# Gate-weight residuals on GpSimd in 1024-wide instead of 256-wide instructions, and one Newton step of a norm moved one head earlier on VectorE

## The chip, the cores and the metric

The kernel runs on one core of a Trainium2 chip. The metric is the device time of one execution in microseconds (us). The profile and the trace are those of one execution; engines are PE (TensorE), DVE (VectorE), ACT (ScalarE), POOL (GpSimd) and SP (SyncE, which issues most of the DMAs).

## The reference

Two trunk layers run over 128 context tokens and 512 latent tokens (640 in all, width 1024). What matters here is the middle of a layer:

```
g = sigmoid(h @ w_gate + b_gate)            # 1024 -> 4 x 1024, four branches
oa = diff_attn(q, ka, va, lam, sa)          # branch A: 4 heads, two score maps each
oa = rms_norm(oa, a_subln_g) * (1 - lam_init)   # per head, over 64 values
ob = neighborhood_attn(...)                 # branch B: 4 heads
oc = softmax_attn(...)                      # branch C: 4 heads
merged = g[0]*oa@a_wo + g[1]*ob@b_wo + g[2]*oc@c_wo + g[3]*od
x += gate1 * (merged @ w_out);  then a mixture of experts, top 2 of 16
```

## The kernel before

The order of the work on each engine is written out by hand; semaphores connect the engines. A float32 matmul is done as three float16 passes (`passes`, L430): each float32 operand is split into a high half (the cast to float16) and a low half (the float32 minus the high half). For a weight block of 128 x 2048 ACT makes the high half (`whi`, in two casts of 1024, L1360), and POOL makes the low half (`wlo`) with `low`: `wlo = wf - whi`, L1719. The operands all lie in SBUF. `low` cuts a block into pieces of `piece` columns and signals `w_lo` after the last; the default is 1024, and the calls for the gate weights pass `piece=256`.

The gate projection has 16 units of 2048 columns a layer (`GATE_UNITS`). It gives 13 such calls a layer on POOL in 256-wide pieces (units 3 to 15). The two buffers `whi` and `wlo` alternate: when PE has finished a unit, ACT casts the unit after the next one into the buffer that came free, and POOL follows.

The gate matmuls are laid out between the attention heads as filler for PE. A tile of 128 query tokens has 12 heads (`HDS`): heads 0 to 3 of branch A with two maps each, then one map for each of heads 4 to 11. The tiles go in the order 1, 2, 3, 4, 0; tile 0 is the context, with 128 keys instead of 640. `GATE_SETS` gives each step `g` (one head) 8 or 4 sets of three passes, 64 a latent tile, which are two gate units. So POOL's blocks fall on the same two places in every latent tile: one in its first heads, one in its later heads.

A step `g` of PE in the later heads of a tile: scores of the next pair of heads (`scores`, L1033), the transposes of the weights of head g-1 (`turn`, L1049), their product with V (`values`), gate sets. `turn` waits for `pt_ready` of the head before, which DVE gives with L2150.

The step `g` of DVE from head 4 on, in this order: `maxima(g + 1)` (L2165, a reduce over PSUM), `weights_turned(g - 1)` (L2150, the low half of the transposed weights, one operand in PSUM), `sub_norm(g - 2)`, `sums(g)` (L2183, a reciprocal). `sub_norm` is the RMS norm of branch A, spread over five heads: head 5 forms the sums of squares, head 6 a first estimate of 1/sqrt and a Newton step, heads 7 and 8 a Newton step each, head 8 the product (L2228), head 9 the gain (L2232). A Newton step (`root_step`) has three instructions on 128 x 4 values in SBUF, L2203, L2205 and L2207, with a drain behind each. In the first heads of a tile `sums` also has L2187 (one column) and L2193 (128 x 640, `wmix`), both with two inputs in SBUF.

The convolution early in a layer (L1999, 128 x 655, both inputs in SBUF) runs on DVE beside `low` in its default pieces of 1024.

Of the kernel before, what the change touches and what calls it, by code (L numbers as in the profile page):

```python
# [47 lines left out]
V_GATE = V_IN + IN_UNITS  # L48
V_WO = V_GATE + GATE_UNITS
V_OUT = V_WO + 2  # L50
V_ALL = V_OUT + OUT_UNITS
# [31 lines left out]
def build(nc, t):  # L83
    ctx = ExitStack()
    with ctx:
# [354 lines left out]
        def ran_before(eng):  # L440


            b, ran = (eng.value_load(loopi[0:1, n:n + 1], min_val=0, max_val=LAYERS * (PAIRS + 1)) for n in (0, 2))
            return b, ran, b + ran
# [12 lines left out]
        def head(g):  # L457

            if not 0 <= g < HEADS_ALL:
                return None  # L460
            ti, hd = divmod(g, HDS)
            return ti, ORDER[ti], hd, ((2 * hd, 2 * hd + 1) if hd < 4 else (hd + 4,))
# [1246 lines left out]
        @block.gpsimd  # L1709
        def _(pool):  # L1710
            for l in range(LAYERS):
                def low(count, j, dst=None, n=2048, piece=1024):

                    pool.wait_ge(w_hi.sem, count)
                    hi = (whi[j] if dst is None else dst[0])[:, 0:n]
                    lo = (wlo[j] if dst is None else dst[1])[:, 0:n]
                    for a in range(0, n, piece):
                        b = min(a + piece, n)
                        ins = pool.tensor_tensor(lo[:, a:b], wf[j][:, a:b], hi[:, a:b], ALU.subtract)  # L1719
                    ins.then_inc(w_lo.sem, 1)  # L1720

                pool.wait_ge(*w_lo(l, V_IN + 2))
                for u in range(2, IN_UNITS):
                    low(l * V_ALL + (V_IN + u + 1), u % 2, n=2048 if u < IN_UNITS - 1 else KC * 160)

                low(l * V_ALL + (V_GATE + 1), 0)
                for n in range(1, TILES):
                    if n >= 3:
                        low(l * V_ALL + (V_GATE + n - 1), (n - 2) % 2)
                    if n == 1:  # L1730
                        pool.wait_ge(*proj_ready(l, 40))
                        pool.wait_ge(*cv_var(l, 1))
                    else:
                        pool.wait_ge(*ab_t(l, 2 * n - 1))
                    v = proj[:, n, 0:512].rearrange("p (h n) -> p h n", n=32)
                    r2 = rope2.rearrange("p (h n) -> p h n", n=32)
                    for o, i in ((0, 8), (8, 0), (16, 24), (24, 16)):
                        pool.tensor_tensor(r2[:, :, o:o + 8], v[:, :, i:i + 8],
                                           sinb[:, n - 1:n, o:o + 8].to_broadcast([P, 16, 8]), ALU.mult)
                    pool.drain()  # L1740
                    pool.tensor_tensor(v, v, cosb[:, n - 1:n, :].to_broadcast([P, 16, 32]), ALU.mult)
                    pool.drain()
                    pool.tensor_tensor(roped.rearrange("p (h n) -> p h n", n=32), v, r2, ALU.add).then_inc(roped_ready.sem, 1)
                low(l * V_ALL + (V_GATE + 4), 1, piece=256)
                with pool.Fori(0, GATE_UNITS // 2 - 2) as i:
                    for j in range(2):
                        low(l * V_ALL + i * 2 + (V_GATE + j + 5), j, piece=256)
                for b in (2, 3, 0, 1):
                    flat = [w[:, b, :, :].rearrange("p k n -> p (k n)") for w in (wohi, wolo)]
                    if b < 2:  # L1750
# [20 lines left out]
                b, ran, past = ran_before(pool)  # L1771
# [30 lines left out]
                for tile in range(TILES):  # L1802
                    for ch, dst in enumerate((cga, cgb)):
                        n = ch * TILES + tile
# [6 lines left out]
        def _(dve):  # L1811
# [62 lines left out]
            def bc(ap, shape):  # L1874
                return ap.to_broadcast(shape)
# [91 lines left out]
            for l in range(LAYERS):  # L1967
# [229 lines left out]
                def root_step(first):  # L2197

                    x, y, t2 = ostat[:, 0, :], ostat[:, 1, :], ostat[:, 2, :]
                    if first:  # L2200
                        dve.tensor_scalar(y.bitcast(I32), x.bitcast(I32), -0.5, 1597463007.0, ALU.mult, ALU.add)
                        dve.drain()
                    dve.tensor_tensor(t2, y, y, ALU.mult)  # L2203
                    dve.drain()
                    dve.scalar_tensor_tensor(out=t2, in0=t2, scalar=-0.5, in1=x, op0=ALU.mult, op1=ALU.mult)  # L2205
                    dve.drain()
                    dve.scalar_tensor_tensor(out=y, in0=t2, scalar=1.5, in1=y, op0=ALU.add, op1=ALU.mult)  # L2207
                    dve.drain()

                def sub_norm(g):  # L2210

                    ti, _, hd, _ = head(g)
                    oa = otok[:, ti % 2, 0:256].rearrange("p (h n) -> p h n", h=4)
                    if hd == 5:
                        dve.wait_ge(*o_ready(l, ti * HDS + 4))
                        dve.tensor_tensor(osq, otok[:, ti % 2, 0:256], otok[:, ti % 2, 0:256], ALU.mult)
                        dve.drain()
                        dve.tensor_reduce(ostat[:, 2, :], osq.rearrange("p (h n) -> p h n", h=4), AX_X, ALU.add)
                        dve.drain()
                        dve.tensor_scalar(ostat[:, 0, :], ostat[:, 2, :], 1.0 / 64, EPS, ALU.mult, ALU.add)  # L2220
                        dve.drain()
                    elif hd == 6:
                        root_step(True)
                    elif hd == 7:
                        root_step(False)
                    elif hd == 8:
                        root_step(False)
                        dve.tensor_tensor(oa, oa, bc(ostat[:, 1, :].rearrange("p (h o) -> p h o", o=1), [P, 4, 64]),  # L2228
                                          ALU.mult)
                        dve.drain()  # L2230
                    elif hd == 9:
                        dve.tensor_tensor(oa, oa, bc(rowg[:, 0:64].rearrange("p (o n) -> p o n", o=1), [P, 4, 64]),  # L2232
                                          ALU.mult).then_inc(on_ready.sem, 1)

                for g in range(-1, HEADS_ALL + 4):
                    last_turned = head(g - 4) and head(g - 4)[2] == HDS - 1
                    if g % HDS < 4:
                        if head(g):
                            sums(g)
                        if last_turned:  # L2240
                            rows_turned(*head(g - 4)[:2])
                        if head(g + 1):
                            maxima(g + 1)
                        if head(g - 1):
                            weights_turned(g - 1)
                    else:
                        if head(g + 1):
                            maxima(g + 1)
                        if head(g - 1):
                            weights_turned(g - 1)  # L2250
                        if head(g - 2):
                            sub_norm(g - 2)
                        if head(g):
                            sums(g)
                    if g > HEADS_ALL:
                        wo_low((2, 3, 0)[g - HEADS_ALL - 1])
# [107 lines left out]
                b, ran, past = ran_before(dve)  # L2364
# [75 lines left out]
                for n, sh in enumerate((1, 2, 4, 8)):  # L2440
                    a, o = csum[n % 2], csum[1 - n % 2]
# [98 lines left out]
                with dve.Fori(0, p + 1) as i:  # L2540
                    for n in range(2):
                        c, j = i * 2 + (1 + n), 1 - n
# [128 lines left out]
```

## Time and profile before

| | us |
|---|---|
| median of 3 runs | 1917.68 |
| lowest, highest | 1914.58, 1923.54 |
| the profiled execution | 1923.54 |
| its span | 1921.7 |

Busy in the span: PE 86%, DVE 63%, ACT 47%, POOL 24%. The mean granted TensorE clock is 0.925 of full speed. A row of the time-ordered view has start, length, engine, line, operation, written and read tiles, and in brackets how long the engine had been idle and who released it. PE's busy time is matmul time; rows of one instruction can overlap a little with the next. An idle engine costs nothing unless it is the one that others end up waiting for.

### The profile page before, as it was taken

What the parts mean: (1) busy time and instruction counts of PE and PEld (TensorE: products, weight loads), DVE (VectorE), ACT (ScalarE), POOL (GpSimd) and SP (SyncE); (2) the same over time, 40 slices, a digit from 0 to 9 for tenths busy, and PEclk for the clock granted to TensorE, in tenths of its full rate; (3) what the DMA queues carried; (4) which work ended last, traced back from release to release, by engine and by line L of the source; (5) the groups of instructions that cost most, each with busy time, mean ns of one, the idle gap of its engine ahead of it and who ended that gap; (6) DMA issues with size and microseconds to landing.
All of it is one profiled execution on the core that took longest, in us unless ns stands there. A gap on an engine that the chain in (4) does not pass through costs nothing.

```text
span 1921.7 us, 34497 instructions
## 1 busy us (share of the span) xinstructions
PE 1657.3 (86%) x13277; PEld 1114.3 (58%) x13277; DVE 1206.4 (63%) x1888; ACT 904.5 (47%) x1478; POOL 455.7 (24%) x430
## 2 busy tenths in 40 slices
PE   6799889999989886888679998999999989288877
PEld 4478766777665443434356876677776546244436
DVE  4595355777438448777575916477773664777754
ACT  3322545666541124777532235466664221376753
POOL 0032252222242023212202315322223121322111
PEclk7899999999999997999869999999999999699995
DMA  8555235532327466999634622322223643399954
GB/s 294 180 198 168 70 130 187 183 106 70 114 96 253 155 244 223 361 373 356 246 117 145 240 85 90 99 100 72 72 79 125 214 150 110 135 356 352 376 216 161
DMA packets 191107, 350.71 MB, mean 183 GB/s; under 512 B 15478, under 2 KB 98935, under 8 KB 190711
## 3 DMA queue, kind: packets, MB, share of 16 engines
q1 hardware_dynamic: 181647, 319.58, 47.5%
q0 software_dynamic: 7776, 28.32, 4.0%
q8 instruction: 97, 1.59, 0.3%
q10 hardware_dynamic: 1543, 0.88, 0.2%
q14 instruction: 44, 0.35, 0.1%
HBM read 287.72 MB, written 61.01 MB: 181 GB/s over the span
## 4 chain that ended last, share of the span: by engine, by line
PE 63%; DVE 12%; DMA 10%; ACT 5%; issue 5%; DVEq 2%; SPq 1%; another core or an unknown queue 0%; ACTq 0%; POOL 0%; POOLq 0%
PE PS L430 36%; PE PS L437 10%; DMA wf<-in_moe_w 4%; DMA arena<-in_moe_w 4%; PE PS L1049 3%; PE PS L1033 3%; PE PS L851 2%; DVE arena L2369 2%; PE PS L807 1%; DMA wf<-in_w_out 1%; PE PS L833 1%; PE PS L817 1%; ACT arena L1615 1%; ACT arena L1433 1%; DVE hpart L1868 1%
## 5 line engine op out<-in xcount | busy, mean ns | idle before, releaser
L1719 POOL TENSOR_TENSOR wlo<-wf,whi 128x256 f16<-128x256 f32 (+1 forms) x268 | 278.3, 1071 | 926.4 <-ACT whi L1360 926.4
L430 PE MATMUL PS<-hpart,whi 128*128 128x320 f16 x2048 | 425.5, 301 | 16.9 <-ACT arena L1433 15.9
L430 PE MATMUL PS<-hpart,wlo 128*128 128x320 f16 x1024 | 307.6, 300 | 0.0
L430 PE MATMUL PS<-whi,hpart 128*128 128x256 f16 (+2 forms) x1568 | 298.3, 291 | 5.9 <-DVE scratch L1989 3.6
L430 PEld LDWEIGHTS PS<-hpart,whi 128*128 128x128 f16 x2048 | 191.2, 98 | 105.9 <-issue 34.9
L430 PE MATMUL PS<-wlo,hpart 128*128 128x256 f16 (+2 forms) x784 | 225.9, 291 | 0.0
L430 PEld LDWEIGHTS PS<-whi,hpart 128*128 128x128 f16 x1568 | 151.9, 98 | 65.3 <-issue 24.1
L2369 DVE TENSOR_TENSOR arena<-arena 128x2048 f16<-128x2048 f32 x66 | 149.5, 2288 | 41.0 <-ACT arena L1615 41.0
L2165 DVE TENSOR_REDUCE stat<-PS 128x1 f32<-128x640 f32 (+1 forms) x160 | 110.7, 713 | 79.7 <-PE PS L1033 77.3
L1433 ACT ACTIVATE arena<-PS,pcol 128x320 f32<-128x320 f32 x128 | 67.5, 527 | 171.8 <-PE PS L430 166.6
L1999 DVE SCALAR_TENSOR_TENSOR scratch<-scratch,cw 128x655 f32<-128x655 f32 x120 | 138.8, 1198 | 4.8 <-issue 0.4
L1615 ACT CAST arena<-arena 128x2048 f16<-128x2048 f32 x66 | 123.4, 1897 | 33.0 <-DMA arena<-in_moe_w 33.0
L1360 ACT CAST whi<-wf 128x1024 f16<-128x1024 f32 (+1 forms) x84 | 109.8, 1307 | 54.1 <-DMA wf<-in_w_out 35.0
L1523 ACT ACTIVATE scratch<-PS,stat 128x640 f32<-128x640 f32 (+1 forms) x160 | 113.0, 709 | 39.2 <-DVE stat L2165 38.5
L430 PEld LDWEIGHTS PS<-hpart,wlo 128*128 128x128 f16 x1024 | 100.6, 98 | 39.8
L2150 DVE TENSOR_TENSOR arena<-PS,arena 128x640 f16<-128x640 f32 (+1 forms) x120 | 85.6, 714 | 49.4 <-ACT arena L1542 46.3
L2369 DVE TENSOR_TENSOR wlo<-wf,whi 128x2048 f16<-128x2048 f32 x36 | 82.3, 2291 | 40.7 <-ACT whi L1615 39.4
L1542 ACT CAST arena<-PS 128x640 f16<-128x640 f32 (+1 forms) x120 | 72.8, 607 | 57.0 <-PE PS L1049 56.8
L430 PE MATMUL PS<-arena,hpart 128*128 128x512 f16 x384 | 95.6, 402 | 4.0 <-issue 3.6
L1398 ACT COPY arena<-PS 128x256 f32<-128x256 f32 (+1 forms) x80 | 28.8, 360 | 144.9 <-PE PS L430 144.9
L430 PE MATMUL PS<-arena,scratch 128*128 128x512 f16 x408 | 93.6, 379 | 2.8 <-DVE scratch L2526 2.8
L437 PE MATMUL PS<-arena,whi 128*128 128x128 f16 (+1 forms) x512 | 91.5, 302 | 0.0
(351 smaller groups left out, 2861.3 us busy)
## 6 DMA issues: line engine op xcount, KB each, us to landing
arena<-in_moe_w SPq DMA_DIRECT2D x66, 1024.0 KB, 8.5
arena<-in_w_ada SPq DMA_DIRECT2D x40, 1024.0 KB, 7.2
wf<-in_moe_w SPq DMA_DIRECT2D x36, 1024.0 KB, 10.2
wf<-in_w_gate SPq DMA_DIRECT2D x32, 1024.0 KB, 5.5
g_rows<-arena SPq DMA_DIRECT2D x128, 160.0 KB, 1.8
wf<-in_w_in SPq DMA_DIRECT2D x18, 1024.0 KB, 7.8
y_rows<-scratch SPq DMA_DIRECT2D x34, 512.0 KB, 9.0
arena<-g_rows SPq DMA_DIRECT2D x24, 640.0 KB, 5.1
```

Of the source, the lines that this page charges most:

```text
L430: ins = pe.matmul(out, st, mv, start=first and n == 0, stop=last and n == 2)
L437: ins = pe.matmul(pr(pair)[:, a:b], st, mv[:, a:b], start=first and n == 0, stop=last and n == 2)
L1360: return act.copy(whi[j][:, a:b] if dst is None else dst, wf[j][:, a:b])
L1433: act.activation(sg(n), bank(7, 320), ACT.Tanh, scale=0.5, bias=pcol[:, PC_BG + u % 4 * 8 + d:PC_BG + u % 4 * 8 + d + 1]).then_inc(g_ready ...
L1523: act.activation(ex[:, m % 4, 0:nk], pr(m % 2)[:, 0:nk], ACT.Exp, bias=stat[:, 0, m:m + 1], accum_out=stat[:, 1, m:m + 1]).then_inc(ex_rea ...
L1542: act.copy(pthi[:, hd % 2, 0:nk], pr(2)[:, 0:nk]).then_inc(pt_hi.sem, 1)
L1615: act.copy(mwhi[3 * j + q], mwf[3 * j + q]).then_inc(mw_hi.sem, 1)
L1719: ins = pool.tensor_tensor(lo[:, a:b], wf[j][:, a:b], hi[:, a:b], ALU.subtract)
L1999: ins = dve.scalar_tensor_tensor(out=zacc[:, c, :], in0=zpad[:, c, k:k + NZ], scalar=cw[:, c, k:k + 1], in1=zacc[:, c, :], op0=ALU.mult, o ...
L2150: dve.tensor_tensor(ptlo[:, hd % 2, 0:nk], pr(2)[:, 0:nk], pthi[:, hd % 2, 0:nk], ALU.subtract).then_inc(pt_ready.sem, 1)
L2165: dve.tensor_reduce(stat[:, 0, m:m + 1], pr(m % 2)[:, 0:nk], AX_X, ALU.max, negate=True).then_inc(mx_ready.sem, 1)
L2369: dve.tensor_tensor(mwlo[3 * j + q], mwf[3 * j + q], mwhi[3 * j + q], ALU.subtract).then_inc((mw_lo2 if q == 2 else mw_lo).sem, 1)
```

## The change

`low` loses its parameter: all pieces are 1024 wide, so a gate unit takes two POOL instructions instead of eight. And the Newton step of head 8 is done in head 7, behind the one that is there, so that head 7 has six small instructions and head 8 none besides the product.

```diff
-                def low(count, j, dst=None, n=2048, piece=1024):
+                def low(count, j, dst=None, n=2048):
...
-                    for a in range(0, n, piece):
-                        b = min(a + piece, n)
+                    for a in range(0, n, 1024):
+                        b = min(a + 1024, n)
                         ins = pool.tensor_tensor(lo[:, a:b], wf[j][:, a:b], hi[:, a:b], ALU.subtract)
...
-                low(l * V_ALL + (V_GATE + 4), 1, piece=256)
+                low(l * V_ALL + (V_GATE + 4), 1)
                 with pool.Fori(0, GATE_UNITS // 2 - 2) as i:
                     for j in range(2):
-                        low(l * V_ALL + i * 2 + (V_GATE + j + 5), j, piece=256)
+                        low(l * V_ALL + i * 2 + (V_GATE + j + 5), j)
...
                     elif hd == 7:
                         root_step(False)
+                        root_step(False)
                     elif hd == 8:
-                        root_step(False)
                         dve.tensor_tensor(oa, oa, bc(ostat[:, 1, :].rearrange("p (h o) -> p h o", o=1), [P, 4, 64]),
                                           ALU.mult)
```

## Rows read from the trace of the kernel before

**Rows 1.** The page: busy time, and the chain that ended last.

```profile
PE 1657.3 (86%) x13277; PEld 1114.3 (58%) x13277; DVE 1206.4 (63%) x1888; ACT 904.5 (47%) x1478; POOL 455.7 (24%) x430
...
PE 63%; DVE 12%; DMA 10%; ACT 5%; issue 5%; DVEq 2%; SPq 1%; another core or an unknown queue 0%; ACTq 0%; POOL 0%; POOLq 0%
```

**Rows 2.** One tile's stretch: length, busy time and count of PE, PEld, DVE, ACT, POOL; clock.

```profile
394.36:442.74 48.38, 47.55 (x538) 34.30 (x537) 36.13 (x69) 32.54 (x69) 10.73 (x17) 1.00 0.25 83
```

**Rows 3.** Instructions in time order, second latent tile, heads 7 and 8 of the norm.

```profile
394.36 5.08 POOL L1719 TENSOR_TENSOR wlo<-wf,whi 128x256 f16<-128x256 f32 x8 [20.11 <-ACT whi L1360]
...
395.94 0.36 DVE L2203 TENSOR_TENSOR ostat<-ostat 128x4 f32<-128x4 f32 x1
...
396.38 0.56 DVE L2205 SCALAR_TENSOR_TENSOR ostat<-ostat 128x4 f32<-128x4 f32 x1
397.01 0.55 DVE L2207 SCALAR_TENSOR_TENSOR ostat<-ostat 128x4 f32<-128x4 f32 x1
...
397.64 0.16 DVE L2183 RECIPROCAL stat<-stat 128x1 f32<-128x1 f32 x1
...
398.44 0.81 DVE L2150 TENSOR_TENSOR arena<-PS,arena 128x640 f16<-128x640 f32 x1
399.17 0.28 DVE L2203 TENSOR_TENSOR ostat<-ostat 128x4 f32<-128x4 f32 x1
399.40 0.74 PE L1049 MATMUL PS<-ident,scratch 128*128 128x128 f32 x5 [0.28 <-DVE arena L2150]
...
399.52 0.16 DVE L2205 SCALAR_TENSOR_TENSOR ostat<-ostat 128x4 f32<-128x4 f32 x1
399.76 0.16 DVE L2207 SCALAR_TENSOR_TENSOR ostat<-ostat 128x4 f32<-128x4 f32 x1
```

**Rows 4.** The same for lines L1999 and L1719, around 1034 us.

```profile
L1999 DVE SCALAR_TENSOR_TENSOR scratch<-scratch,cw x120: 886/902/2840, 100.1 to 1104.8; 128x655 f32<-128x655 f32 x120
...
L1999 DVE SCALAR_TENSOR_TENSOR scratch<-scratch,cw x1: 2607/2607/2607, 1034.2 to 1034.2; 128x655 f32<-128x655 f32 x1
L1719 POOL TENSOR_TENSOR wlo<-wf,whi x2: 2290/2505/2720, 1033.9 to 1036.1; 128x1024 f16<-128x1024 f32 x2
L1999 DVE SCALAR_TENSOR_TENSOR scratch<-scratch,cw x1: 2757/2757/2757, 1036.8 to 1036.8; 128x655 f32<-128x655 f32 x1
```

**Rows 5.** A block in two 1024-wide pieces with DVE out of the way.

```profile
L1719 POOL TENSOR_TENSOR wlo<-wf,whi 128x1024 f16<-128x1024 f32 x2 | 4.2, 2128 | 14.8 <-ACT whi L1360 14.8
```

**Rows 6.** Time order, the other block of the tile, first heads.

```profile
416.97 5.65 POOL L1719 TENSOR_TENSOR wlo<-wf,whi 128x256 f16<-128x256 f32 x8 [17.54 <-ACT whi L1360]
...
420.88 1.22 DVE L2193 SCALAR_TENSOR_TENSOR scratch<-scratch,cfa 128x640 f32<-128x640 f32 x1
421.36 0.80 ACT L1532 CAST arena<-PS 128x768 f16<-128x768 f32 x1
422.19 0.96 DVE L2173 TENSOR_TENSOR arena<-PS,arena 128x768 f16<-128x768 f32 x1
```

**Rows 7.** Time order, the first heads of the context tile.

```profile
511.71 5.12 POOL L1719 TENSOR_TENSOR wlo<-wf,whi 128x256 f16<-128x256 f32 x8 [15.51 <-ACT whi L1360]
...
515.79 0.96 DVE L2173 TENSOR_TENSOR arena<-PS,arena 128x768 f16<-128x768 f32 x1 [1.37 <-ACT arena L1532]
```

**Rows 8.** Time order, head 7 of the last latent tile of layer 0.

```profile
491.12 5.07 POOL L1719 TENSOR_TENSOR wlo<-wf,whi 128x256 f16<-128x256 f32 x8 [20.11 <-ACT whi L1360]
...
494.75 0.16 DVE L2183 RECIPROCAL stat<-stat 128x1 f32<-128x1 f32 x1 [0.42 <-issue]
```

**Rows 9.** Stretches around two pauses of PE (columns as in rows 2).

```profile
252.68:254.95 2.27, 0.00 (x1) 0.01 (x1) 2.19 (x9) 2.24 (x3) 0.23 (x1) 1.00 0.29 88
254.95:258.00 3.05, 3.05 (x25) 2.54 (x26) 3.05 (x7) 2.11 (x7) 1.91 (x4) 1.00 1.00 305
...
264.47:267.30 2.83, 0.00 (x0) 0.00 (x1) 2.75 (x8) 0.53 (x1) 1.13 (x1) 1.00 0.49 195
267.30:271.10 3.80, 3.80 (x18) 2.95 (x19) 3.39 (x7) 1.77 (x5) 2.28 (x5) 0.57 0.09 36
```

## The prediction

> **What bounds the kernel now.** I read the page first [rows 1]. PE is busy for 86% of the span and has 63% of the chain that ended last; POOL, whose instructions the change rewrites, has 0% of that chain, and DVE, where the other edit is, has 12%. So a cheaper POOL buys nothing by itself, and DVE counts only where PE waits for it. Next I took the busy time by stretches over the attention heads, where the 256-wide pieces lie. One latent tile takes 48.38 us and PE is busy for 47.55 us of them [rows 2]; the same stretch repeats within 0.1 us through both layers. PE has 0.83 us of idle time a tile: little to win, and no room to absorb a new stall. Then I read one such tile in time order. POOL makes two blocks a tile at fixed places: one just before heads 7 and 8 of the norm [rows 3], one in the first heads of the next tile [rows 6].
>
> What to see in rows 3: the three instructions of a Newton step (L2203, L2205, L2207) handle 4 values a partition and take 0.16 us each when POOL is quiet, 0.24 us from start to start (the pair at 399.52 and 399.76). While POOL runs they take 0.36, 0.56 and 0.55 us and end at 396.30, 396.94 and 397.56. POOL's eight pieces take 5.08 us, one each 0.63 us, and the third, fourth and fifth end at about these three times. Each tiny instruction has waited for the piece that was running, and POOL had started the next piece before the following one could go. Instructions with one operand in PSUM (L2150, 0.81 us) show no such wait.
>
> **Does the wait grow with the piece?** The convolution shows it, for there the pieces are already 1024 wide [rows 4]. L1999 takes 0.90 us alone. The one at 1034.24 takes 2.61 us, beside a piece that runs from 1033.86 for 2.29 us; the next takes 2.76 us, beside the second piece, which ends at 1038.85. So a DVE instruction waits for a whole 1024-wide piece, and POOL's second piece gets in ahead of the second DVE instruction. The Trainium skill, SBUF — State Buffer, section "SBUF: two separate sides", says this as a rule: the port pair that DVE and GpSimd share is an exclusive lock, held for the whole instruction, and a DVE instruction with two SBUF inputs needs it against a GpSimd one that reads SBUF. By that rule, the trace agrees. It speaks against this change; if the loser only shared bandwidth, four times the piece would cost DVE nothing more and the sum below would be near zero.
>
> **The change part by part.**
>
> POOL's work: a block goes from 5.08 us in eight pieces to 4.2 us in two of 2.13 us that end 4.2 us after the first starts [rows 5]. That is 0.9 us on each of 26 blocks. PE needs a block only when it has used up the other buffer, half a tile (24 us) later, and the loads that the block's end releases are as far ahead. I cost this at nothing; the cover is those 24 us.
>
> Wider pieces with the moved step, at the seven ordinary places (four latent tiles in two layers make eight; the last of layer 0 comes below). I take POOL's start of rows 3, since ACT's cast that releases it stands in ACT's own order just ahead of the cast that leads to L2150. Piece one ends at 394.36 + 2.13 = 396.49. L2203, issued at 395.94, ends with it: 396.50. Piece two runs until 394.36 + 4.2 = 398.56. L2205 is issued at 396.6 and ends with that: 398.57. L2207 ends 0.24 us later, at 398.81 (before: 397.56, so 1.25 us later from the width alone). Then come three more instructions, 3 x 0.24 = 0.72 us: 399.53. The reciprocal L2183 starts 0.08 us after that as it does now: at 399.61 instead of 397.64, 1.97 us late.
>
> Who waits for that: behind it in DVE's order stand the next reduce and L2150, which ended at 399.25 and would now end at 401.22. PE's transposes L1049 at 399.40 had already waited 0.28 us for it, so nothing covers the delay: PE stalls 1.97 us more. Head 8's step is indeed shorter by its three instructions (0.28 + 0.24 + 0.24 us), but they stood behind L2150, in a stretch where PE was not waiting for DVE; taking them from there returns nothing, while in head 7 they stand in front. 7 x 1.97 = 13.8 us.
>
> The eighth place [rows 8]: L2183 had an idle 0.42 us in front of it. By the same count it starts at 491.12 + 5.25 = 496.37 instead of 494.75: 1.6 us.
>
> The other block of the latent tiles [rows 6]: the one-column L2187 just ahead of L2193 waits in both versions, now for piece two, which ends at 416.97 + 4.2 = 421.17. L2193 then runs unhindered from 421.25, some 0.9 us as L1999 of nearly the same width does [rows 4], until 422.15 (before: 420.88 + 1.22 = 422.10). L2173 behind it also waits for ACT's cast, which ends at 422.16. So L2173 and the PE transposes that wait for it move by 0.05 us: six places, 0.3 us.
>
> The context tile's first heads [rows 7]: L2187 ends with piece one, at 513.84, and L2193 with piece two, 511.71 + 4.2 = 515.91, plus about 0.2 us; L2173 moves from 515.79 to about 516.15, and PE waits for it: 2 x 0.35 = 0.7 us.
>
> The remaining eight blocks (in each layer the last two, and two at the beginning of the heads) meet DVE where it idles in between, or where fewer waits and longer ones cancel. A wait of 0.4 us, as L2205 has now over its 0.16 us, can go or come at each: within 3 us either way in all; I take zero.
>
> Sum: 13.8 + 1.6 + 0.3 + 0.7 = 16.4 us. The profiled execution took 1923.54 us with a span of 1921.7, so it would take 1939.9. It was the slowest of the three, 5.9 us over the median; against the median I predict 1917.68 + 16.4 = 1934.1 us, 0.86% more.
>
> What is not in the trace: six tiny instructions in a row beside 1024-wide pieces. The lower bound is one waited piece instead of two, 1 us in all (rival C works it out); a gain is excluded, for the first wait and the six instructions stand on the path in any case. The upper bound is both pieces as priced and 0.2 us more at each place, as L2193 and the second L1999 end some way behind their piece: 18 us. I take the two pieces, for the rows nearest to it, rows 3 for the size of the instruction and rows 4 for the size of the piece, show every instruction waiting.
>
> **The rivals.**
>
> A. Forecast: each of two tiny instructions waits for a whole piece, PE stalls; 1934.1.
>
> B. The same, and PE's clock falls. PE would pause for 0.28 + 1.97 = 2.25 us each time. In one place PE pauses for 2.27 us and the granted clock stays 1.00; in another it pauses for 2.83 us and the clock is then 0.57 over 3.80 us (the 1.2 GHz level for most of it) [rows 9], a loss of 3.80 x 0.43 = 1.6 us. Eight such losses add 13 us: 1947. For it: 2.25 lies not far under the pause that cost clock. Against: the pause of 2.27 us is as long and did no harm. The Trainium skill, TensorE: Matmul & The Clock Gate, section "What's actually happening", says that the clock goes by how busy the array has been recently, so the same pause can fare differently by what stands around it; by that rule some of the eight could pay.
>
> C. DVE gets its second instruction in before POOL's second piece. Then only L2203 waits for piece one (396.50), the other five take 5 x 0.24 = 1.2 us and are through at 397.70, against 397.56 now: 0.14 us a tile, 1 us in all, so not slower. It decides at the gap between two pieces: L2205 must be ready within it. Against: L2205 now comes 0.08 us behind L2203's end and yet waits for a whole piece each time [rows 3], as does the second L1999 [rows 4]. Time: 1919.
>
> D. PE doesn't pay in full, since a later wait of PE shrinks in turn. It could give back at most its 0.83 us of idle time a tile: 16.4 - 8 x 0.83 = 9.8 us, 1927.5. If more of the delay falls where PE has other work in front of it, down to 1922.
>
> E. Faster, since DVE loses fewer waits in all: bounded by PE's idle 0.83 us a tile, eight tiles, 6.6 us or 0.35%. It can't pass 0.5%.
>
> **How the numbers follow.** A 0.60, B 0.13 (with some of the eight places paying), C 0.09, D 0.15, E 0.03. A change under 0.5% (9.6 us) is about what a measurement of this kernel can't tell from none. A's own range, with its bounds and the spread of the medians, is 1929 to 1940. The whole range, from D's lower part to the smaller half of B, is 1922 to 1943. Slower by over 0.5%: A and B and a good part of D, less A's chance to be measured low: 0.78. Within: C and the rest of D: 0.19. Faster: 0.03.
>
> **What would show it.** In the profile of the changed kernel: L1719 with 26 x 2 = 52 instructions of 1024 where there were 208 of 256; in rows like rows 3, L2203 at about 0.55 us and the L2205 behind it at about 2.0 us, then four at 0.16; L1049 with an idle time of about 2.2 us released by L2150; a tile of 50.4 us with PE's busy time still 47.55 and the clock 1.00. If L2205 there takes 0.16 us, C is right; if L1049's idle time stays under 1 us, D; if the clock in these tiles is under 1.00, B. The prediction is wrong above all if POOL's start moves against L2203 by more than 0.5 us, for then the tiny instructions meet only one of the pieces.

## The result, and the profile after

The changed kernel takes 1948.40 us (median of 4 runs, 1934.07 to 1952.65), the kernel before 1919.99 us (median of 4). The ratio is 1.0138, with a 95% interval of 1.0098 to 1.0178: slower, by about 26 us. All 21 recorded executions of the changed kernel have a median of 1945.89 us and reach from 1934.07 to 1961.12. The prediction was slower by 16.4 us, 1934.1 us with a range of 1922 to 1943. The direction was right, and the time lies above the range, by either median. The profiled execution took 1945.07 us, with a span of 1943.2.

The page of the kernel after: busy time and the chain that ended last. POOL has 25 us less work than in [rows 1], and L2205, an instruction on four values a partition, has 1% of the chain that ended last, and did not stand among its leading entries before.

```profile
PE 1672.5 (86%) x13277; PEld 1120.0 (58%) x13277; DVE 1220.6 (63%) x1888; ACT 904.7 (47%) x1478; POOL 430.2 (22%) x274
...
PE PS L430 36%; PE PS L437 10%; DMA arena<-in_moe_w 4%; DMA wf<-in_moe_w 3%; PE PS L1033 3%; PE PS L1049 3%; PE PS L851 2%; DVE arena L2369 2%; PE PS L807 1%; DMA wf<-in_w_out 1%; PE PS L833 1%; PE PS L817 1%; DVE ostat L2205 1%; ACT arena L1615 1%; ACT arena L1433 1%
```

The kernel after in time order, the same place as [rows 3]:

```profile
398.44 4.22 POOL L1719 TENSOR_TENSOR wlo<-wf,whi 128x1024 f16<-128x1024 f32 x2 [21.54 <-ACT whi L1360]
...
400.03 0.56 DVE L2203 TENSOR_TENSOR ostat<-ostat 128x4 f32<-128x4 f32 x1
...
400.67 2.01 DVE L2205 SCALAR_TENSOR_TENSOR ostat<-ostat 128x4 f32<-128x4 f32 x1
...
402.76 0.16 DVE L2207 SCALAR_TENSOR_TENSOR ostat<-ostat 128x4 f32<-128x4 f32 x1
402.99 0.16 DVE L2203 TENSOR_TENSOR ostat<-ostat 128x4 f32<-128x4 f32 x1
...
403.71 0.16 DVE L2183 RECIPROCAL stat<-stat 128x1 f32<-128x1 f32 x1
...
405.47 0.74 PE L1049 MATMUL PS<-ident,scratch 128*128 128x128 f32 x5 [2.25 <-DVE arena L2150]
```

This is the predicted picture to within 0.03 us: L2203 waits for piece one, L2205 for piece two, four instructions run free, the reciprocal starts 5.27 us after POOL's start (predicted 5.25), and PE's pause is 2.25 us (2.25 to 2.27 us at six of the eight places, 2.61 at two). So where does the rest come from? The stretches tell. In the rows below, each stretch runs from POOL's block in the later heads of a tile to the next block (columns as in [rows 2]); the eight such stretches of the kernel after:

```profile
346.48:372.68 26.20, 23.94 (x260) 17.41 (x258) 17.35 (x33) 15.14 (x33) 4.22 (x3) 0.93 0.42 147
...
398.44:423.04 24.60, 22.34 (x260) 16.44 (x258) 17.34 (x33) 15.04 (x33) 4.22 (x2) 1.00 0.27 92
423.04:448.81 25.77, 25.21 (x282) 17.87 (x279) 20.01 (x36) 17.51 (x37) 4.23 (x3) 1.00 0.21 68
448.81:476.64 27.83, 25.57 (x260) 18.00 (x258) 17.34 (x33) 15.14 (x33) 4.22 (x3) 0.88 0.20 62
...
502.40:526.54 24.14, 21.29 (x223) 15.70 (x222) 12.57 (x35) 11.95 (x34) 4.22 (x3) 0.93 0.32 101
...
1289.27:1314.23 24.96, 22.35 (x260) 16.43 (x258) 17.35 (x33) 15.04 (x33) 4.23 (x3) 1.00 0.23 70
...
1339.99:1367.75 27.76, 25.50 (x260) 18.08 (x258) 17.35 (x33) 15.14 (x33) 4.22 (x3) 0.88 0.20 63
...
1393.51:1421.36 27.85, 25.59 (x260) 17.66 (x258) 17.36 (x33) 15.04 (x33) 4.22 (x2) 0.88 0.20 63
...
1447.13:1469.35 22.22, 19.72 (x223) 15.05 (x222) 12.56 (x35) 11.95 (x34) 4.22 (x3) 1.00 0.38 125
```

The row at 423.04 is the other half of a tile, for comparison; before, it took 25.77 us too. The first and the last of the eight before:

```profile
345.98:368.59 22.61, 22.34 (x260) 16.43 (x258) 16.20 (x33) 15.04 (x33) 5.07 (x9) 1.00 0.48 170
...
1423.54:1443.77 20.23, 19.71 (x223) 15.04 (x222) 11.42 (x35) 11.94 (x34) 5.07 (x8) 1.00 0.42 137
```

With the clock at 1.00 a full stretch takes 24.60 us against 22.61: 1.99 us for the pause. With 0.93 it takes 26.20, 1.60 us more, with 0.88 it takes 27.8, 3.2 us more, and in these PE's busy time itself has grown, from 22.34 to 23.94 and 25.57 us for the same 260 matmul rows. The eight sum to 205.56 us against 176.51, 29.05 us more, and PE's busy time in them grew by 12.8 us. That is rival B, at five of the eight places. The span grew by 21.5 us only: single executions also differ elsewhere (the four of the kernel before range over 9 us and the profiled one was the slowest of them); the ratio says 26.

The two places with a pause of 2.61 us are the last of layer 0 and the first of layer 1. In each DVE has an idle time of about 0.42 us between two of the small instructions:

```profile
507.31 0.16 DVE L2203 TENSOR_TENSOR ostat<-ostat 128x4 f32<-128x4 f32 x1 [0.42 <-issue]
...
509.78 0.74 PE L1049 MATMUL PS<-ident,scratch 128*128 128x128 f32 x5 [2.61 <-DVE arena L2150]
...
1294.42 0.16 DVE L2205 SCALAR_TENSOR_TENSOR ostat<-ostat 128x4 f32<-128x4 f32 x1 [0.43 <-issue]
```

### The profile page after: what moved, and what is told of

Its sections match the earlier page's. It is cut to its first block, busy times and chain, and to the rows that moved or that the text cites. A ratio compares the mean times of both kernels' runs of the same rounds, so it can differ in the third digit from the quotient of the medians.

```text
span 1943.2 us, 34341 instructions
## 1 busy us (share of the span) xinstructions
PE 1672.5 (86%) x13277; PEld 1120.0 (58%) x13277; DVE 1220.6 (63%) x1888; ACT 904.7 (47%) x1478; POOL 430.2 (22%) x274
## 4 chain that ended last, share of the span: by engine, by line
PE 62%; DVE 13%; DMA 10%; ACT 6%; issue 5%; DVEq 2%; SPq 1%; POOL 0%; ACTq 0%; POOLq 0%
PE PS L430 36%; PE PS L437 10%; DMA arena<-in_moe_w 4%; DMA wf<-in_moe_w 3%; PE PS L1033 3%; PE PS L1049 3%; PE PS L851 2%; DVE arena L2369 2%; PE PS L807 1%; DMA wf<-in_w_out 1%; PE PS L833 1%; PE PS L817 1%; DVE ostat L2205 1%; ACT arena L1615 1%; ACT arena L1433 1%
## 5 line engine op out<-in xcount | busy, mean ns | idle before, releaser
L1719 POOL TENSOR_TENSOR wlo<-wf,whi 128x1024 f16<-128x1024 f32 x112 | 250.6, 2258 | 974.2 <-ACT whi L1360 974.2
L430 PE MATMUL PS<-hpart,whi 128*128 128x320 f16 x2048 | 431.7, 304 | 16.9 <-ACT arena L1433 15.9
L1999 DVE SCALAR_TENSOR_TENSOR scratch<-scratch,cw 128x655 f32<-128x655 f32 x120 | 138.8, 1198 | 4.8 <-issue 0.4
L2150 DVE TENSOR_TENSOR arena<-PS,arena 128x640 f16<-128x640 f32 (+1 forms) x120 | 85.6, 714 | 48.2 <-ACT arena L1542 45.1
L430 PE MATMUL PS<-arena,hpart 128*128 128x512 f16 x384 | 99.6, 415 | 4.0 <-issue 3.6
L1049 PE MATMUL PS<-ident,scratch 128*128 128x128 f32 x504 | 78.5, 281 | 24.8 <-DVE arena L2150 19.2
```

Source lines behind the costliest of these rows:

```text
L430: ins = pe.matmul(out, st, mv, start=first and n == 0, stop=last and n == 2)
L1049: ins = pe.transpose(pr(2)[:, c * P:(c + 1) * P], src[:, c * P:(c + 1) * P], ident[:, :])
L1999: ins = dve.scalar_tensor_tensor(out=zacc[:, c, :], in0=zpad[:, c, k:k + NZ], scalar=cw[:, c, k:k + 1], in1=zacc[:, c, :], op0=ALU.mult, o ...
L2150: dve.tensor_tensor(ptlo[:, hd % 2, 0:nk], pr(2)[:, 0:nk], pthi[:, hd % 2, 0:nk], ALU.subtract).then_inc(pt_ready.sem, 1)
```

## The experiments

In what follows "the eight stretches" are these, from POOL's block in the later heads to the next block; 176.51 us in the kernel before. They are those of one profiled execution of each kernel. Each ratio is against executions of the kernel before that were made together with that experiment's (medians 1916.18, 1916.86 and 1912.83 us).

**Wide pieces alone.**

```diff
 # against the changed kernel
                     elif hd == 7:
                         root_step(False)
-                        root_step(False)
                     elif hd == 8:
+                        root_step(False)
```

> Only the pieces are 1024 wide; head 8 keeps its Newton step. Theory (whole-piece waits, and a clock that falls only behind the longer pauses): L2203 about 0.56 us and L2205 about 2.0 us beside POOL, the reciprocal 1.25 us later than before, PE's pause ahead of L1049 0.28 + 1.25 = 1.53 us. A pause of 1.72 us in the kernel before cost no clock, so the clock stays 1.00 in these tiles: 8 x 1.25 + 1.0 = 11 us over the kernel before, ratio 1.006. Rival (the clock falls behind any new stall here): half of the eight places lose 1.6 us or more as well, 18 us or more, ratio 1.009 or more.

Measured: ratio 1.0062 (1.0030 to 1.0094). In time order:

```profile
396.03 2.01 DVE L2205 SCALAR_TENSOR_TENSOR ostat<-ostat 128x4 f32<-128x4 f32 x1
...
400.11 0.74 PE L1049 MATMUL PS<-ident,scratch 128*128 128x128 f32 x5 [1.54 <-DVE arena L2150]
```

The stretch of that place:

```profile
393.81:417.68 23.87, 22.33 (x260) 16.42 (x258) 17.33 (x33) 15.04 (x33) 4.21 (x2) 1.00 0.28 94
```

The pause is 1.54 us (1.90 at the last place of layer 0), the clock is 1.00 in all eight stretches, and they sum to 186.63 us, 10.1 more than before. That is as the theory had it: the width costs about 1.25 us a place and, in this execution, no clock.

**The moved step alone.**

```diff
 # against the kernel before
                     elif hd == 7:
                         root_step(False)
+                        root_step(False)
                     elif hd == 8:
-                        root_step(False)
```

> Only the Newton step is moved; the pieces stay 256 wide. Theory: six instructions wait for one piece each (0.63 us), the last for the eighth piece, 5.08 us after POOL's start: the reciprocal 1.9 us later than before, nearly the 1.97 of both parts together, PE's pause 2.15 us. So 8 x 1.9 = 15 us without any loss of clock (ratio 1.008), and up to 1.014 if the pause of 2.15 us costs clock as often as that of 2.25 us. Rival (the parts simply add, 0.72 us a place for the moved step): 6 us, ratio 1.003.

Measured: ratio 1.0154 (1.0118 to 1.0191).

```profile
402.57 0.55 DVE L2207 SCALAR_TENSOR_TENSOR ostat<-ostat 128x4 f32<-128x4 f32 x1
...
403.20 0.55 DVE L2203 TENSOR_TENSOR ostat<-ostat 128x4 f32<-128x4 f32 x1
403.82 0.56 DVE L2205 SCALAR_TENSOR_TENSOR ostat<-ostat 128x4 f32<-128x4 f32 x1
404.46 0.55 DVE L2207 SCALAR_TENSOR_TENSOR ostat<-ostat 128x4 f32<-128x4 f32 x1
...
406.84 0.74 PE L1049 MATMUL PS<-ident,scratch 128*128 128x128 f32 x5 [2.15 <-DVE arena L2150]
```

One of the stretches with a lower clock:

```profile
346.44:374.16 27.72, 25.56 (x260) 17.77 (x258) 17.24 (x33) 15.13 (x33) 5.08 (x8) 0.88 0.40 138
```

Each of the six waits for one piece; PE pauses 2.15 us, as expected, and the clock falls in seven of the eight stretches of the profiled execution, which sum to 32.5 us more. The ratio lies a little above the expected 1.008 to 1.014, and its interval covers the upper end. This one edit costs as much as both together: the two don't add. The rival of 0.72 us a place is out.

**The pause filled.** PE does matmuls while it would stand still; nothing reads their result.

```diff
 # against the changed kernel, PE, at the head step before L1049's late start
+                    if g % HDS == HDS - 1 and 0 < g < HEADS_ALL - HDS:
+                        pe.wait_ge(*ex_ready(l, g // HDS * MAPS + MAPS - 1))
+                        for _ in range(10):
+                            pe.matmul(PS[:, 0, 640:1024], hhi[:, 0, 0:P], hhi[:, 1, 0:384], start=True, stop=True)
```

> The changed kernel, and in the pause PE does ten matmuls of 384 columns (1.6 us at full clock) whose result nobody reads, ahead of L1049 in the four places of a layer. Theory (the 10 us above the predicted 16 are TensorE's clock): DVE's rows stay as they are, L1049 starts as late as in the changed kernel, the clock is 1.00 in all eight tiles, and the time is the predicted 16.4 us over the kernel before, ratio 1.0086, with a smaller spread between executions. Rival (the excess comes from another wait): ratio stays at 1.013 or goes above it.

Measured: ratio 1.0071 (1.0044 to 1.0099). In time order, and one stretch (the lines of DVE are 4 higher in this kernel):

```profile
400.05 1.79 PE L1068 MATMUL PS<-hpart 128*128 128x384 f16 x10
...
402.46 0.74 PE L1049 MATMUL PS<-ident,scratch 128*128 128x128 f32 x5 [0.63 <-DVE arena L2154]
```

```profile
445.80:470.39 24.59, 23.96 (x270) 17.41 (x268) 17.33 (x33) 15.02 (x33) 4.22 (x2) 1.00 0.22 71
```

L1049 starts as late after POOL's start as in the changed kernel (7.01 us against 7.03), but PE's idle time in front of it is down to 0.63 us (0.98 at two places), the clock is 1.00 in all eight stretches, and none takes over 24.94 us. They sum to 192.67 us, 16.16 more than before. So 16.2 us of the 29.05 are the pauses themselves and 12.9 us are the clock, which agrees with the 12.8 us by which PE's busy time had grown. Adding work to PE has taken 13 us away; the two ratios, 1.0138 and 1.0071, are as far apart.

**The pause half filled,** with four matmuls instead of ten.

```diff
 # against the kernel with the filled pause
-                        for _ in range(10):
+                        for _ in range(4):
```

> As the filled pause, with four of the unread matmuls (0.65 us) instead of ten, so that PE is idle for about 1.5 us of the pause, as with wide pieces alone, but DVE is as late as in the changed kernel. Theory (what counts is how long PE is idle, 1.5 us costs nothing): clock 1.00 in all eight stretches, each 24.60 us, ratio 1.007 to 1.009. Rival (half-filled pauses cost clock too): some stretches below 1.00 and over 26 us, ratio 1.011 or more.

Measured: ratio 1.0094 (1.0057 to 1.0132), with a clock of 1.00 in six stretches. In two, where DVE was some 0.35 us later than elsewhere, PE was idle for 1.96 and 1.95 us instead of 1.6, and the clock was 0.93 and 0.94. One of the two, the pause and what follows:

```profile
505.62:507.58 1.96, 0.00 (x1) 0.03 (x1) 1.89 (x5) 0.78 (x2) 0.00 (x0) 1.00 0.01 4
507.58:511.40 3.82, 3.81 (x36) 2.63 (x37) 2.49 (x10) 2.24 (x9) 0.00 (x0) 0.71 0.12 43
```

The expectation that half filling is enough held for the pauses of 1.6 us and failed for the two near 2, though the pause of 1.90 us with wide pieces alone had lost nothing. The ratio lies between the two expected ranges and its interval covers both.

**No Newton step in head 7, two in head 8.** Once with the wide pieces, once with the narrow ones.

```diff
 # against the kernel before; the wide version has the changed kernel's `low` as well
                     elif hd == 7:
-                        root_step(False)
+                        pass
                     elif hd == 8:
                         root_step(False)
+                        root_step(False)
```

> Pieces of 1024, head 7 without a Newton step, head 8 with two, behind L2150. Theory: no DVE instruction with two SBUF inputs is issued while POOL runs there, L1049's idle time goes from 0.28 (before) and 2.25 us (changed) to nearly 0, and two Newton steps (1.44 us) fit into DVE's idle time: the time is that of the kernel before or up to 4 us less, ratio 0.998 to 1.001. Rival (wide pieces cost by themselves, wherever the small instructions stand): ratio 1.005 or more.

> Pieces of 256 as before, head 7 without a Newton step, head 8 with two. Theory: head 7 has nothing that POOL can hold; the two steps of head 8 are issued when one or two pieces are still to come, behind L2150, where PE waits for nothing: the same stretches as with wide pieces and the late steps (22.15 us), ratio 0.998 to 1.001. Rival (narrow pieces are what protects DVE): a difference of over 2 us from the wide pieces with late steps, one way or the other.

Measured: ratio 0.9996 (0.9974 to 1.0018) with wide pieces, 1.0000 (0.9973 to 1.0027) with narrow ones. The stretch of the one and of the other:

```profile
440.61:462.75 22.14, 22.14 (x260) 16.51 (x258) 15.16 (x33) 15.02 (x33) 4.22 (x2) 1.00 0.25 78
```

```profile
439.57:461.71 22.14, 22.14 (x260) 16.50 (x258) 15.59 (x33) 15.02 (x33) 5.08 (x8) 1.00 0.24 78
```

PE is never idle in these two stretches, L1049's wait for L2150 is gone at all eight places, and both sum to 172.41 us, 4.1 less than before. In the time of the whole kernel that can't be told from nothing. With the steps placed there, the width of the pieces makes no difference, as the theory had it. By the ratios both versions are 1.4% under the changed kernel and can't be told from the kernel before.

**A third Newton step in head 7.** The norm gets one step more than it needs.

```diff
 # against the changed kernel
                     elif hd == 7:
                         root_step(False)
                         root_step(False)
+                        root_step(False)
```

> The changed kernel with one more Newton step in head 7 (three there; the result of the norm gets one step more than it needs). Theory: 0.72 us more DVE work in each of eight places, PE's pause about 2.97 us instead of 2.25. The kernel before had a pause of 2.83 us, and the clock fell behind it: so the clock falls at all eight places, not at five. 22 us of pauses and 8 x 1.6 to 3.3 us of clock: 35 to 48 us over the kernel before, ratio 1.018 to 1.025. Rival (what the clock does is chance, not tied to the pause's length): 5.8 us over the changed kernel, ratio 1.016 or 1.017, and about five places with a loss.

Measured: ratio 1.0187 (1.0131 to 1.0243), inside the expectation, but not for its reason. The pauses are 2.97 us as worked out (3.31 at one place), and the clock fell at four of the eight places only. The eight stretches sum to 30.7 us more than before, under the expected 35 to 48. One place where it did not fall:

```profile
404.75:407.72 2.97, 0.00 (x0) 0.03 (x1) 2.58 (x9) 0.78 (x2) 0.00 (x0) 1.00 0.00 0
407.72:411.50 3.78, 3.78 (x45) 2.70 (x46) 1.99 (x5) 2.15 (x7) 0.00 (x0) 1.00 0.12 43
```

So the theory that a longer pause costs clock for certain is wrong, and its rival, with about five places, is nearer. The ratio can't decide between them, as its interval covers the rival's 1.016 as well.

**Pieces of 512.**

```diff
 # against the changed kernel
-                    for a in range(0, n, 1024):
-                        b = min(a + 1024, n)
+                    for a in range(0, n, 512 if n == 2048 and dst is None else 1024):
+                        b = min(a + (512 if n == 2048 and dst is None else 1024), n)
```

> The changed kernel with pieces of 512 in all of GpSimd's blocks of whole weight units. Theory: six waiting instructions are held until the block is done whatever its cut is: L2203, L2205 and L2207 wait for pieces two, three and four of about 1.1 us each (estimate between the 0.63 us of a 256 and the 2.08 us of a 1024 piece), the last ends 4.5 us after POOL's start, the rest is free; PE's pause 2.2 to 2.35 us, ratio 1.010 to 1.016 as with 1024. Rival (a piece half as wide holds half as long): pause about 1.3 us and ratio 1.004.

Measured: ratio 1.0185 (1.0126 to 1.0244).

```profile
401.72 0.70 DVE L2203 TENSOR_TENSOR ostat<-ostat 128x4 f32<-128x4 f32 x1
...
402.50 1.04 DVE L2205 SCALAR_TENSOR_TENSOR ostat<-ostat 128x4 f32<-128x4 f32 x1
...
403.61 1.04 DVE L2207 SCALAR_TENSOR_TENSOR ostat<-ostat 128x4 f32<-128x4 f32 x1
...
407.20 0.74 PE L1049 MATMUL PS<-ident,scratch 128*128 128x128 f32 x5 [2.30 <-DVE arena L2150]
```

Three instructions wait for one piece each, the last until the block is done. The pause is 2.30 us, about that of 256 (2.15) and 1024 (2.25). The clock fell at all eight places here, and the stretches sum to 35.9 us more than before, so the ratio is above the expected range. (The edit also narrows POOL's blocks of 2048 columns outside the gate projection; the eight stretches hold only gate blocks.)

**The changed kernel profiled twice more,** with no edit.

> The changed kernel once more, unchanged, for one look. If the clock's losses are a matter of how the pause happens to lie, the eight stretches of the later heads lose at other places, and in another number, than in the first look (five of eight: 0.93, 1.00, 0.88, 0.93, 1.00, 0.88, 0.88, 1.00). If they are tied to the place and the length of the pause, the same five lose.

> The changed kernel a third time: as in the look before it. Chance: again another set of places. Tied to the place: the same set. In either case the pauses themselves are 2.25 us, and the time goes with the number of stretches at the lower clock, 1.6 us for each 3.4 us of it.

Measured: 1953.31 and 1941.99 us. The clock of the eight stretches, in order (four of layer 0, then four of layer 1):

| profiled execution | layer 0 | layer 1 |
|---|---|---|
| first | 0.93, 1.00, 0.88, 0.93 | 1.00, 0.88, 0.88, 1.00 |
| second | 0.93, 1.00, 0.88, 0.93 | 0.88, 0.88, 1.00, 1.00 |
| third | 1.00, 0.88, 0.88, 0.93 | 1.00, 0.88, 0.88, 1.00 |

Two of the changed places of the second execution, and two of the third:

```profile
1297.45:1325.60 28.15, 25.55 (x260) 18.10 (x258) 17.33 (x33) 15.12 (x33) 4.21 (x2) 0.88 0.20 62
...
1404.98:1429.57 24.59, 22.34 (x260) 16.43 (x258) 17.34 (x33) 15.03 (x33) 4.21 (x3) 1.00 0.23 71
```

```profile
344.30:368.89 24.59, 22.33 (x260) 16.43 (x258) 17.33 (x33) 15.04 (x33) 4.22 (x2) 1.00 0.45 156
...
394.66:422.48 27.82, 25.57 (x260) 18.03 (x258) 17.34 (x33) 15.14 (x33) 4.22 (x3) 0.88 0.25 82
```

Each execution has five places with a loss, but not the same five: four places lost in one execution and are clean in another. Neither expectation holds in full, though: the number was five each time, three places lost in all three executions and one in none, so the place may matter as well as chance. Three executions can't separate the two. The eight stretches sum to 29.0 and 30.8 us more than before. The pauses are the same each time. The expectation that the time goes with the number of these places was not borne out: these two sums differ by under 2 us and the times by 11, the other way round. The rest of the kernel varies as well; what varies there is not shown.

## Why the prediction was wrong, and where it was right

- *A DVE instruction waits for a whole piece, and POOL gets its next piece in first.* Right, with pieces of 256, 512 and 1024: a small instruction that meets a whole piece takes 0.55, 1.04 and 2.01 us instead of 0.16. By the rule of the Trainium skill (SBUF — State Buffer, "SBUF: two separate sides"), an exclusive lock for a whole instruction, the trace agrees. Rival C, L2205 slipping in between, is refuted by the 2.01 us.
- *L2183 1.97 us late, nothing covers it, PE stalls as much.* Right: a clean stretch is 1.99 us longer, and with the pause filled the eight are 16.16 us longer, against 13.8 + 1.6 = 15.4 predicted. The missing 0.7 us: I took DVE's idle 0.42 us of [rows 8] as covering part of the delay, but it stayed, between two of the small instructions, so that PE's pause there was 2.61 us (the L1049 at 509.78); and the first place of layer 1, ordinary before, got such an idle time too and became 2.34 us longer instead of 1.97. What DVE does in these 0.42 us the profile doesn't show; nor did the prediction have a reason for where they fall.
- *The rest small.* The stretch of [rows 7] grew by 0.27 us in layer 0 and 0.20 in layer 1, predicted 0.35 each; that of [rows 6] by 0.00, predicted 0.05. POOL's saved 25 us came back nowhere, as costed. Rival D is refuted: PE gave nothing back. Rival E is out by the interval.
- *The step that failed: A against B.* The sum put the clock at nothing, for the reason that "the pause of 2.27 us is as long and did no harm", and B got 0.13. What the runs showed: in three profiled executions of the changed kernel pauses of 2.25 to 2.61 us lost clock at 15 of 24 places, 1.6 or 3.2 us a place. In the first of the three that is 12.9 us, shown to be the clock by PE's busy time (12.8 us more for the same matmuls) and by the filled pause. Of B's own working, 8 x 1.6 = 13 us was near in sum by luck, by two errors that cancel: five places, not eight, but three of them at the double price. One harmless pause of one execution could not exclude an outcome that differs from place to place and from execution to execution. The upper bound of 18 us was a bound on DVE's delay alone and left the clock out. The range should have reached at least B's 1947.
- *The parts.* I priced the moved step as 0.72 us on top of the width's 1.25. The sum is right for both together, but it isn't a property of the parts: alone, the moved step makes a pause of 2.15 us, 1.87 us more than the 0.28 before.

## What to carry to other kernels

Before a small instruction with two SBUF inputs is put beside a GpSimd block, count how many such instructions are issued while the block runs: each waits for one piece, and enough of them wait for the whole block, whatever the cut. Move them, as here behind the work that PE waits for, rather than tune the piece. And where PE is the bound, price a new pause twice, once as its length and once as the clock it may cost; if it can't be removed, cheap filler matmuls in it were worth 13 us here, when there were enough of them (ten; with four, two of the eight places still lost clock).

## What was not expected of the hardware

The same pause, in the same kernel and execution, can cost clock or not. In the kernel after, one pause and what follows, and another:

```profile
403.22:405.47 2.25, 0.00 (x1) 0.03 (x1) 2.09 (x6) 0.79 (x2) 0.00 (x0) 1.00 0.00 0
405.47:409.20 3.73, 3.73 (x45) 2.67 (x46) 1.94 (x5) 2.10 (x6) 0.00 (x0) 1.00 0.12 44
453.57:455.84 2.27, 0.01 (x2) 0.03 (x1) 2.09 (x6) 0.78 (x2) 0.00 (x0) 1.00 0.00 0
455.84:459.60 3.76, 3.76 (x33) 2.46 (x34) 0.40 (x3) 1.53 (x5) 0.00 (x0) 0.52 0.14 48
459.60:463.00 3.40, 3.40 (x14) 1.91 (x13) 3.21 (x8) 1.66 (x4) 0.00 (x0) 0.52 0.00 0
```

After the first the array stays at its 2.4 GHz level, after the second it is at the 1.2 GHz level for nearly all of 7 us. Over all profiled executions at these places: pauses of 1.5 to 1.6 us lost nothing at 13 places; of 1.9 to 2.0 us, two lost and one didn't; at 2.15 us seven of eight (the moved step alone) and at 2.3 to 2.7 us eight of eight (pieces of 512); at 2.25 to 2.6 us fifteen of 24; at 3.0 to 3.3 us four of eight. So none of 13 below, and 36 of 51 from 1.9 us on; among these the counts don't show that a longer pause is worse, but all save the fifteen of 24 and the pauses under 2 us are from one execution each. What decides between two equal pauses stays open; nothing here was varied but the length and what fills it.
